# Two-layer mLSTM and convolution trunk on one core: gate rows stacked, spreads by transposes, a head's two products in split form

## The reference, cut to what matters

```python
hn = rms_norm(x, norm_w)
u  = hn @ w_in + b_in                 # 2048 x 20496 weights, split among the branches
q, k = silu(depthwise_conv(u_q, u_k)) # width 5
# per head and direction, in closed form over all 256 positions:
g   = cumsum(log_sigmoid(f));  m = running max of (i - g)
s   = (q @ k.T) * dh**-0.5 * exp(i - g - m)     # masked to the past (or the future)
h   = (s @ v) / max(|sum(s)|, exp(-g - m))      # both directions are added
ya  = rms(sigmoid(o) * h) * norm_w * silu(z_a)
c   = depthwise_conv(glu, width 31) -> layer_norm -> silu, * silu(z_b)
x   = x + (sigmoid(g_a) * (ya @ w_a) + sigmoid(g_b) * (c @ w_b)) @ w_out
out = rms_norm(x, final_norm_w)       # after the last layer
```

## Time and profile before

| | |
|---|---|
| median of 3 runs | 2440.14 us (2438.82 to 2440.4) |
| the profiled execution's own time | 2439.07 us |
| its span, first to last instruction | 2437.1 us |
| TensorE busy | 2419.9 us (99%) |
| VectorE busy | 1921.4 us (79%) |
| ScalarE busy | 1365.1 us (56%) |
| mean granted TensorE clock | 0.999 of full |

### The profile page before, as it was taken

The page is one execution under the profiler, slowest core; times in us unless marked ns, Lnnn a source line. Parts: engine busy times, 40 slices in busy tenths (PEclk is TensorE's granted clock), DMA queues, the critical chain, the costliest instruction groups (busy, mean ns, idle before and its releaser), DMA issues.

```text
span 2437.1 us, 38380 instructions
## 1 busy us (share of the span) xinstructions
PE 2419.9 (99%) x13988; PEld 2125.5 (87%) x13988; DVE 1921.4 (79%) x2896; ACT 1365.1 (56%) x1632; POOL 73.5 (3%) x45
## 2 busy tenths in 40 slices
PE   8999999999999999999999999999999999999998
PEld 7888888888888888888888888888888888888887
DVE  7798989898888786556678888888898878765565
ACT  6655454545465557555566654545454655665554
POOL 1000000000000000000000000000000000000000
PEclk9999999999999999999999999999999999999999
DMA  7566656556556666665656665656565666666654
GB/s 215 174 192 179 178 177 178 177 173 180 173 177 190 190 183 193 192 189 182 199 150 197 195 187 169 181 168 181 169 183 167 191 190 190 181 198 190 189 189 139
DMA packets 448170, 444.61 MB, mean 182 GB/s; under 512 B 18000, under 2 KB 445792, under 8 KB 448096
## 3 DMA queue, kind: packets, MB, share of 16 engines
q1 hardware_dynamic: 448096, 443.74, 61.1%
HBM read 441.59 MB, written 2.10 MB: 182 GB/s over the span
## 4 chain that ended last, share of the span: by engine, by line
PE 99%; DVE 0%; DMA 0%; ACT 0%; issue 0%; SPq 0%; ACTq 0%
PE ps L1442 58%; PE ps L1445 29%; PE ps L1460 5%; PE ps L1464 2%; PE px L1603 1%; PE px L1624 1%; PE px L1515 0%; PE ps L1670 0%; PE px L1547 0%; PE px L1611 0%; DMA M<-in_x_dram 0%; PE px L1500 0%; PE ps L1672 0%; PE px L1580 0%; DVE X L813 0%; PE px L1595 0%
## 5 line engine op out<-in xcount | busy, mean ns | idle before, releaser
L1442 PE MATMUL ps<-Hs,W 128*128 128x512 f32 x4960 | 1547.0, 393 | 0.0
L775 DVE TENSOR_TENSOR W<-RAW,W 128x1024 fp32r<-128x1024 f32 x832 | 1018.7, 1230 | 438.8 <-ACT W L425 435.8
L425 ACT CAST W<-RAW 128x1024 fp32r<-128x1024 f32 x832 | 865.3, 1049 | 835.1 <-PE ps L1445 721.0
L1445 PEld LDWEIGHTS ps<-Hs,W 128*128 128x128 f32 x4960 | 932.1, 188 | 205.8
L1445 PE MATMUL ps<-Hs,W 128*128 128x256 f32 x4960 | 979.4, 279 | 0.0
L1442 PEld LDWEIGHTS ps<-Hs,W 128*128 128x128 f32 x4960 | 752.8, 188 | 3.4 <-issue 2.3
L922 DVE SCALAR_TENSOR_TENSOR ACC<-CP,CWT,ACC 128x256 f32<-128x256 f32 x928 | 387.9, 477 | 0.1
L1442 PE MATMUL ps<-YC,W 128*128 128x512 f32 x1152 | 358.7, 393 | 2.6 <-DVE W L775 2.6
L1445 PEld LDWEIGHTS ps<-YC,W 128*128 128x128 f32 x1152 | 216.6, 188 | 47.8
L1445 PE MATMUL ps<-YC,W 128*128 128x256 f32 x1152 | 227.6, 279 | 0.0
L1442 PEld LDWEIGHTS ps<-YC,W 128*128 128x128 f32 x1152 | 174.9, 188 | 2.9 <-DVE W L775 2.8
(11 more groups left out here) (216 smaller groups left out, 1020.6 us busy)
## 6 DMA issues: line engine op xcount, KB each, us to landing
RAW<-in_w_in_dram SPq DMA_DIRECT2D x640, 512.0 KB, 3.7
RAW<-in_w_a_dram SPq DMA_DIRECT2D x64, 512.0 KB, 3.4
RAW<-in_w_b_dram SPq DMA_DIRECT2D x64, 512.0 KB, 3.3
RAW<-in_w_out_dram SPq DMA_DIRECT2D x64, 512.0 KB, 4.3
M<-in_x_dram SPq DMA_DIRECT2D x2, 1024.0 KB, 7.7
HEAD<-in_b_in_dram SPq DMA_DIRECT2D x8, 256.0 KB, 4.5
out_dram<-M SPq DMA_DIRECT2D x4, 256.0 KB, 3.2
out_dram<-M SPq DMA_DIRECT2D x2, 512.0 KB, 4.8
```

The costliest lines, as they stand in the source:

```text
L425: nc.scalar.copy(WH[:, c, :, :], RAW[:, c, :, :]).then_inc(hi_made, 1)
L775: v.tensor_tensor(WL[:, c, :, :], RAW[:, c, :, :], WH[:, c, :, :].bitcast(F32), ALU.subtract).then_inc(lo_made, 1)
L1442: mm(ps[:, 2 * q + t, :], WH[:, c, kk, t * P:t * P + P], act_in[:, kt, :], start=(kt == 0), stop=False)
L1445: i = mm(ps[:, 2 * q + t, S:2 * S], WL[:, c, kk, t * P:t * P + P], act_in[:, kt, 0:S], start=False, stop=(kt == KT - 1))
```

## The change

1. Scores: ScalarE computes the SiLU of each duo of q and k tiles twice, once rounded into a high part and once whole; VectorE subtracts (`qk_low`, four per head) to get a low part. TensorE then does, for each former product, three in fp32r: high by high, high by low, low by high. It waits for `qk_lo` instead of `qk_silu`.
2. Weighted sums of values: the same, with `VH` and `AH` copied by ScalarE and `VL` and `AL` subtracted by VectorE; TensorE waits for `a_lo` and `v_lo`. The parts live in `MX`, which lies over `M`.
3. `spread_columns` is a transpose per column instead of a multiplication by the identity.
4. The running maxima's spread reads 128 rows instead of 40.
5. The gate rows are picked and reversed by four multiplications per layer; four row blocks are stacked at partitions 0, 32, 64 and 96 and turned by one transpose per half.

```diff
@@ ScalarE, in a head @@
+                        nc.scalar.activation((KH, QH)[i // 2][:, duo, :], b, ACT.Silu)
                         nc.scalar.activation(b, b, ACT.Silu).then_inc(qk_silu, 1)
...
+                    act.wait_ge(v_made, u + 2)
+                    nc.scalar.copy(VH, VS).then_inc(v_hi, 1)
                     split_rest(n, 7, 0, 1)
                     sigmoid_out(n, 6, SO_[:, 0:2, :], o_sig)
-                    split_rest(n, 7)
+                    split_rest(n, 7, 1, 2)
+                    act.wait_ge(a_made, u + 1)
+                    nc.scalar.copy(AH, QB[:, 0:ST, :]).then_inc(a_hi, 1)
+                    split_rest(n, 7, 2)
@@ VectorE, in a head @@
+                    def qk_low(i):
+                        dve.wait_ge(qk_silu, u * 4 + (i + 1))
+                        at = slice(2 * (i % 2), 2 * (i % 2) + 2)
+                        whole, high, low = ((K_, KH, KL), (QB, QH, QL))[i // 2]
+                        v.tensor_tensor(low[:, at, :], whole[:, at, :], high[:, at, :].bitcast(F32),
+                                        ALU.subtract).then_inc(qk_lo, 1)
...
                     with_taps(3, 2, 3)
+                    qk_low(2)
                     dve.wait_ge(qk_summed, u * 4 + 3)
                     pair_out(n, 3, QPAD[:, :, 2:2 + S])
                     narrow_conv(3, QB[:, 2:4, :], 2)
-                    with_taps(4, 3, 9)
+                    split_lo(n + 5, 0)
+                    conv_taps(duo, 3, 5)
+                    split_lo(n + 5, 1)
+                    conv_taps(duo, 5, 7)
+                    split_lo(n + 5, 2)
+                    qk_low(3)
+                    conv_taps(duo, 7, 9)
+                    split_lo(n + 5, 3)
...
-                    with_taps(7, 20, 24, 1)
+                    split_lo(n + 8, 1)
+                    dve.wait_ge(v_hi, u + 1)
+                    v.tensor_tensor(VL, VS, VH.bitcast(F32), ALU.subtract).then_inc(v_lo, 1)
+                    conv_taps(duo, 20, 22)
+                    split_lo(n + 8, 2)
+                    dve.wait_ge(a_hi, u + 1)
+                    v.tensor_tensor(AL, QB[:, 0:ST, :], AH.bitcast(F32), ALU.subtract).then_inc(a_lo, 1)
+                    conv_taps(duo, 22, 24)
+                    split_lo(n + 8, 3)
@@ TensorE @@
             def spread_columns(bank, at, columns, done):
-                    i = mm(px[:, bank, at + s * P:at + (s + 1) * P],
-                           columns[:, s:s + 1].to_broadcast([P, P]), IDENT[:], start=True, stop=True)
+                    i = nc.tensor.transpose(px[:, bank, at + s * P:at + (s + 1) * P],
+                                            columns[:, s:s + 1].to_broadcast([P, P]), IDENT[:])
...
+                    for kind in range(2):
+                        dst = px[0:2 * H, 2, kind * S:(kind + 1) * S]
+                        mm(dst, PICK[:, kind, :], GATES, start=True, stop=False)
+                        i = mm(dst, PICK[:, kind + 2, :], GATES[:, ::-1], start=False, stop=True)
...
-                    for b, rows in enumerate((C_R, CB_R, N_R, ROWS[:, 1, :])):
-                        at = (b // 2) * 4 * ST * H + s * 4 * H + (b % 2) * 2 * H
-                        i = mm(px[:, 3, at:at + 2 * H], rows[:, s * P:(s + 1) * P],
-                               IDENT[0:2 * H, 0:2 * H], start=True, stop=True)
+                    i = nc.tensor.transpose(px[:, 3, s * P:(s + 1) * P], STACK[:, s * P:(s + 1) * P],
+                                            IDENT[:])
...
-                    mm(px[:, 1, :], HCUR[:].to_broadcast([MROWS, P]), MR,
+                    mm(px[:, 1, :], HCUR[:].to_broadcast([P, P]), MR,
...
-                    pe.wait_ge(qk_silu, u * 4 + 4)
+                    pe.wait_ge(qk_lo, u * 4 + 4)
                     for s in range(ST):
                         for k in range(HT):
-                            i = mm(px[:, 0, s * S:(s + 1) * S], K_[:, k, s * P:(s + 1) * P],
-                                   QB[:, k, :], start=(k == 0), stop=(k == HT - 1))
+                            mm(dst, KH[:, k, at], QH[:, k, :], start=(k == 0), stop=False)
+                            mm(dst, KH[:, k, at], QL[:, k, :], start=False, stop=False)
+                            i = mm(dst, KL[:, k, at], QH[:, k, :], start=False, stop=(k == HT - 1))
...
-                    pe.wait_ge(a_made, u + 1)
-                    pe.wait_ge(v_made, u + 2)
+                    pe.wait_ge(a_lo, u + 1)
+                    pe.wait_ge(v_lo, u + 1)
```

More of the change, by code:

```diff
@@ L56 @@
 LOW_AT = 32
+ROW_STEP = 32
 MROWS = LOW_AT + 2 * H
@@ L160, in build_trunk @@
         KV_ = K_
+        KH, KL, QH, QL = (MX[:, HT * i:HT * (i + 1), :] for i in range(4))
+        VH, VL = (MX[:, HT * i:HT * (i + 1), :].rearrange("p (s a) b -> p s (a b)", s=ST)
+                  for i in range(2))
+        AH, AL = QH[:, 0:ST, :], QL[:, 0:ST, :]
         GW = M[:, 2 * HT, :].rearrange("p (k g) -> p k g", k=KT)
         GLOW, GATES = M[0:2 * NG, 2 * HT + 1, :], M[0:2 * NG, 2 * HT + 2, :]
-        F_R, A_R, I_R, G_R, C_R, CB_R, Z_R, N_R = (M[0:2 * H, i, :] for i in range(8))
-        MR = GS[0:MROWS, :, :, :].rearrange("p k a g -> p (k a g)")
+        F_R, A_R, I_R, G_R, Z_R, N_R = (M[0:2 * H, i, :] for i in range(6))
+        STACK = M[:, 2 * HT + 3, :]
+        C_R, CB_R, EN_R, ENB_R = (STACK[ROW_STEP * i:ROW_STEP * i + 2 * H, :] for i in range(4))
+        MR = GS[:, :, :, :].rearrange("p k a g -> p (k a g)")
         XROWS = M[:, :, :].rearrange("p (s a) b -> p s (a b)", s=ST)
@@ L572, in _ @@
                 act.wait_ge(m_made, l + 1)
-                nc.scalar.activation(ROWS[:, 1, :], ROWS[:, 1, :], ACT.Exp)
-                nc.scalar.activation(N_R, N_R, ACT.Exp).then_inc(rows_made, 1)
+                both = STACK[2 * ROW_STEP:3 * ROW_STEP + 2 * H, :]
+                nc.scalar.activation(both, both, ACT.Exp).then_inc(rows_made, 1)
                 with act.Fori(2, N_GLU // 2) as j:
@@ L855, in _ @@
             v.reciprocal(R4[:, 0:ST], R4[:, 0:ST]).then_inc(inv_made, 1)
-            steps.mark(v.tensor_tensor(HSEL[:, 0:H], IDENT[0:MROWS, 0:H], IDENT[0:MROWS, H:2 * H], ALU.add))
+            for group, half in enumerate((0, 0, H, H)):
+                steps.mark(v.tensor_copy(PICK[:, group, half:half + H], SEL[:, group * H:(group + 1) * H]))
+            steps.wait()
+            dve.sem_inc(sel_made, 1)
+            steps.mark(v.tensor_tensor(HSEL[:, 0:H], IDENT[:, 0:H], IDENT[:, H:2 * H], ALU.add))
             for at in (LOW_AT, LOW_AT + H):
                 steps.wait()
-                steps.mark(v.tensor_tensor(HSEL[:, 0:H], HSEL[:, 0:H], IDENT[0:MROWS, at:at + H],
+                steps.mark(v.tensor_tensor(HSEL[:, 0:H], HSEL[:, 0:H], IDENT[:, at:at + H],
                                            ALU.add))
@@ L981, in _ @@
                 split_lo(n0 + 3, 2)
[L982 to L986, removed]
                 split_lo(n0 + 3, 3)
@@ L1052, in _ @@
                 steps.wait()
-                for d, rows in enumerate((ROWS[:, 0, :], ROWS[:, 0, ::-1])):
+                for d, rows in enumerate((TOP[:], TOP[:, ::-1])):
                     i = v.scalar_tensor_tensor(out=MR[LOW_AT:MROWS, d * S:(d + 1) * S], in0=rows,
@@ L1549, in _, with sort_gates @@
                 i.then_inc(gates_mm, 1)
-                def turn_gates():
+                def sort_gates():
                     pe.wait_ge(sel_made, 1)
                     pe.wait_ge(gates_made, l + 1)
[L1555 to L1569, removed]
+                    for kind in range(2):
+                        dst = px[0:2 * H, 2, kind * S:(kind + 1) * S]
+                        mm(dst, PICK[:, kind, :], GATES, start=True, stop=False)
+                        i = mm(dst, PICK[:, kind + 2, :], GATES[:, ::-1], start=False, stop=True)
+                    i.then_inc(grows_mm, 1)
+                multiply(n0, 2, Hs, h_lo, l * 4, late=sort_gates)
                 multiply(n0, 3, Hs)
```

61 lines of the change are left out of this document (35 added, 26 removed).

## The result

The changed kernel takes 2483.75 us (median of 4 runs, 2482.82 to 2483.85) against 2440.07 before: a ratio of 1.018 with a 95% interval of 1.0164 to 1.0195, 43.7 us slower. Forecast were 2475 us and a range of 2450 to 2492.

What follows compares the result with a forecast made beforehand. TensorE, busy 99% of the span, was taken as the bound. Waits of 35.2 and 12.8 us plus 13.6 of clock falls, less 26.3 saved, made it 35.3 us slower: 2475 us, range 2450 to 2492.

Steps and rivals of the forecast that it cites:

- The wait for the scores: Before each head's scores: TensorE waits 4.4 us for VectorE's last low part of q and k, 35.2 us in all.
- that before the sums: Before each head's weighted sums of values: TensorE waits 1.6 us for VectorE's low parts, 12.8 us over 8 heads.
- One fall behind each wait for the scores: After each head's 4.4 us stop before the scores: TensorE's clock falls, costing 1.7 us each, 13.6 us in all.
- (e): Layer 0, behind the 16 small instructions: the clock's fall to 0.67 of full over 5.2 us goes, saving 1.7 us.
- What TensorE saves: All TensorE savings together, from products, spreads, maxima, small instructions, a clock fall and gate rows: 26.3 us.
- the products': Scores and weighted sums: three fp32r products replace each float32 one, 6.90 us a head becoming 5.57, 10.7 us saved.
- The small pieces: Savings outside the split products: spreads 5.4 us, maxima 3.2, small instructions 3.7, clock fall 1.7, gate rows 1.6.
- With the clock up: Rival: the waits before scores and sums come but the clock stays up, 2462 us; chance 0.2.
- Falls behind the second wait too: Rival: the clock also falls behind the wait before the weighted sums, 13.6 us more, 2489 us; chance 0.2.
- The short products: Rival: short fp32r products in a row take 0.19 us each, adding 28 us, 2503 us; chance 0.06.
- The faster case: Rival: VectorE has the low parts ready in time for both products, so 26.3 us faster, 2414 us; chance 0.04.

## Why the prediction was right

**The direction and the two waits** came out as argued. The wait for the scores was forecast at 4.4 us a head and is 4.6 at the longest, 36.5 in all (35.2 forecast); that before the sums 1.6, 13.1 in all (12.8). The low parts' place in the order, the second SiLU's 0.54 on ScalarE and the vanished idle 0.60 all stand in VectorE's timeline. The runs with the parts early show that the waits are the cause: with both gone the same kernel is 68 us faster. A head's pass, forecast at 126.1 us, is 127.5 from the first head's scores to the second's (264.32 to 391.83) and 126.8 and 126.7 to the third's and fourth's.

**The clock.** One fall behind each wait for the scores, 13.6 us, was forecast. There is one in each of the eight heads, and they cost 15.2. None behind the stops of 1.6 us was forecast, and there were none, neither in the change nor with those stops alone. The ground for both was thin: one fall in two cases after 1.88 us. The later runs show how thin. The same 16 small multiplications let the clock fall in layer 0, in layer 1 or in both, and a fall followed three of eight stops of 1.9 us. For the stops of 4.4 us the guess was good, for those of 1.6 there was some luck in it. For the same reason the 1.7 us of (e) are a part of the saving that comes and goes from one execution to the next.

**What TensorE saves** was forecast as 26.3 us. It is 24.2 by the medians in the kernel with both parts early, and 2439.07 - 2414.48 = 24.6 by the profiled executions. The term that was too large is the products': 10.7 forecast, 9.1 measured. A short fp32r product in a row of them takes 0.12, not 0.116, so a head's 48 take 5.74 us, not 5.57, which is 1.4 us in eight heads. The small pieces were forecast at 15.6 and are 15.5 (transposes 5.4 against 5.3, the maxima 3.2 against 0.40 a head, so 3.2). The Trainium skill ("TensorE: Matmul & The Clock Gate", Back-to-back issue gap) has 109 ns for 256 columns, as the gap of a single product; the trace's 0.12 disagrees, and the measurement decides.

**What was left out** are the first products behind a stop: 0.39 instead of 0.12 in the sums, and in the first head's scores 0.58 instead of 0.21. At the sums' 0.27 for each of the 16 stops of the two kinds, that is 4.3 us. The account of the change is then, all from runs and traces: 49.6 of waits, 15.2 of clock, 4.3 of first products, less 24.6, so 44.5 us, against 2483.72 - 2439.07 = 44.65 between the profiled executions. The forecast's 35.3 missed 1.7 in the savings, 4.3 in the first products, 1.6 in the waits and 1.6 in the clock. All four misses make the change slower, so none hid another.

**The rivals.** With the clock up the time would have been 2462 by the forecast; the clock was not up. With the stop filled and the clock up it was 2470, because waits and first products were dearer than forecast and the saving smaller. Falls behind the second wait too (2489) are out, since none stands there. The short products did not run at 0.19: at full clock they keep 0.12. The faster case, parts in time, was not the change but a few moved lines from it; I had put its gain at 26.3 us and it is 24.2.

## What to carry to other kernels

Busy sums of 87% on a helping engine say that work fits, not that a result is ready; where an engine works strictly in order, count what stands ahead of the instruction that releases the bottleneck, from the last point at which both are tied. A stop on TensorE costs its length, its first product, and, from some length on, the products behind it at half clock, so two cheap steps placed a few microseconds too late can turn a gain of 24 us into a loss of 44. And when one wait is taken away, look at the next: idle time that it gave another engine goes with it.

## What the runs showed of the hardware beyond what was expected

- The granted clock falls to half behind all eight stops of TensorE of 4.6 us (the change) and all eight of 2.4 to 2.5 us (the last low part two places earlier), behind three of eight of 1.8 to 1.9 us, and behind none of 1.6 us (eight each in the change, with the part one place earlier, with the stop filled, and with the short addition). It goes down while TensorE still waits, as in the change's first head, or when the products have begun again, as in its second. The falls cost the change 1.9 us a head (15.2 / 8).
- The first product behind a stop takes 0.39 us instead of 0.12 at full clock.
- A `split_lo` of VectorE that begins during GpSimd's addition of 128x1024 ends 1.08 or 1.09 us behind the addition's end, whenever it began: it took 1.82 us in the change, 2.79 and 2.81 in the two runs with parts early, and 1.22 when the addition was cut to an eighth and over before it. One that begins just ahead of the addition keeps its 1.21 to 1.23, and then the addition ends 2.26 or 2.27 us behind it. In these traces the two so look as if they took turns. The Trainium skill ("GPSIMD Engine Reference", Specifications) says that the two share SBUF interfaces and contend where VectorE reads two tensors from SBUF, as a `split_lo` does; the trace agrees, with 1.6 us for one such instruction.
- A product that reads 40 of 128 rows took 0.42 us, and the two behind it 0.67; with 128 rows 0.23 and 0.46.
